# Reordering the front of a decoder layer: memory matmuls between tile 1's attention groups, queries behind them

## The chip, the cores and the metric

One Trainium2 chip, one core. The metric is the device time of one execution in microseconds (us), lower is better. TensorE (PE) works on a 128 by 128 array, with VectorE (DVE), ScalarE (ACT), GpSimd (POOL) and the DMA queue of SyncE (SP) beside it; each takes its instructions in the order in which the program issues them, and they meet at semaphores.

## The reference

A layer over 256 positions of width 1024, in two sub-layers, each closed with `LayerNorm(alpha * x + f(x))`:

```python
# mixing: one projection of x gives all heads; outputs are concatenated and projected
nsa  = g0 * attend(q, compress(k), compress(v)) + g1 * attend(q, selected blocks) + g2 * attend(q, window)
dsa  = attend(q, k, v over the 64 keys with the largest index score)
mem  = softmax(q @ mem_k.T / 8) @ mem_v          # 4 heads, 256 memory tokens
x1   = layer_norm(alpha * x + concat(nsa, dsa, mem) @ w_out)
# channel: PEER, 8 retrieval heads over 128 * 128 experts
s1, s2 = (x1 @ w_query) halves @ sub_keys ; top 16 of each, top 16 of their sums -> experts, gates
y    = sum_e gate_e * gelu(x1 @ u_e) * v_e
out  = layer_norm(alpha * x1 + y)
```

With 256 positions the selection takes all blocks and the window reaches over all keys, so both branches are plain causal attention with their own keys and values.

## The kernel before

Tokens lie in two tiles of 128 (t = 0 and 1). All matrix work of the front is float32, which the trace shows as two matrix instructions for each matmul of the program. The kernel has a **front** (projections, attention, output projection, first norm, the queries of PEER) up to about 284 us and then 128 **expert chunks** in (`expert_in`) and 128 out (`expert_out`); the change touches only the front. The order on each engine is written out by hand.

**Groups.** Attention other than the compressed branch is cut into 20 groups (`UNITS`), each at most 512 score columns wide: in tile 0 "sel" and "win" for two kv groups with four heads each, "dsa" in two halves, "mem" in two halves; in tile 1 the same with two heads a group. A group u runs through

- `scores(u)` on PE (L573 and after), which may start once `maxima(u-2)` has read the PSUM bank,
- `maxima(u)` on DVE (L1298, L1302, L1306): adds the mask and takes each row's maximum,
- `exps(u)` on ACT (L927): the exponential with its row sum,
- `normalise(u)` on DVE (L1314, L1317, L1321): multiplies by one over the sum and, for sel and win, by the gate,
- `turn(u)` on PE (L619): two or four transposes into PSUM bank 2, and `save_turn(u)` on ACT (L937) copies them out,
- `outputs(u)` on PE: probabilities times values into banks 6 and 7.

PE's loop issues `scores(u+2)`, `turn(u)`, then whatever else is laid there, then `outputs(u)`, so that the something else covers ACT's copy.

**Laid between them before.** A generator `filler` holds the last projections of tile 1 and the six memory projections `memory(0)` to `memory(5)` (queries, keys and values of the memory heads, 8 steps each); all of it is spent by the end of group 5. Then come `compress_hidden` (32 matmuls with 30 columns each, issued in one piece after `turn(6)`), `index_later` (index scores of tile 1), `compress_kv`, the compressed branch (`cmp_scores`, `cmp_turn`, `cmp_out`), the output projection of tile 0 (`mix(0)`, 16 steps of 512 columns, spread in fours over groups 9, 10, 12 and 11), the transposes of the normed tile (`turn_x1(0)`) after group 14's turn, and queries 0 to 9 beside groups 15 to 19. After group 19 follow queries 10 and 11, the output turns and `mix(1)`, queries 12 to 15, `turn_x1(1)` and queries 16 to 31. The experts start after that.

**DVE's order** follows the groups: `normalise(u)`, then `maxima(u+2)`, and between them rotary embedding of tile 1 (`rope(1)`), `compress_input`, `index_sum` (eight passes that sum the index heads, L1220), eight `index_round`s a tile that mark the top 64, the compressed softmax (`cmp_shift`, L1266 to L1272; `cmp_probs`, L1277 to L1287), the norm of tile 0, and the top 16 of sub-key scores (`subkey_tops`).

**SP** loads the query weights through a ring of 7 slots (`load_query`).

Of the kernel before, what the change touches and what calls it, by code (L numbers as in the profile page):

```python
# [19 lines left out]
KD = D // P  # L20
# [66 lines left out]
def constants():  # L87
# [8 lines left out]
    for at, half in ((0, 8), (8, 4)):  # L96
# [33 lines left out]
         + [(0, "dsa", 0, EVEN), (0, "dsa", 0, ODD), (0, "mem", 0, EVEN), (0, "mem", 0, ODD)]  # L130
         + [(1, kind, g, hs) for kind in ("sel", "win") for g in range(2) for hs in PAIRS]
# [5 lines left out]
TURNS = ([("u", u) for u in range(9)] + [("o", 0, 1), ("u", 9), ("u", 10), ("u", 11), ("o", 0, 0)]  # L137
         + [("u", u) for u in (12, 13, 14)] + [("x", 0, 0), ("x", 0, 1)] + [("u", u) for u in range(15, NU)]
         + [("o", 1, 0), ("o", 1, 1), ("x", 1, 0), ("x", 1, 1)])
QUERY_AT = 15  # L140
# [3 lines left out]
def peer_layer_kernel(nc, x, xT, memT, positions, w_tok, w_memq, w_memk, w_memv, w1k, w1v, w2k, w2v, peT,  # L144
                      w_out, ln1, wq, subk, uT, pv, ln2, consts, out):
    with ExitStack() as ctx:
# [42 lines left out]
        def small(n):  # L189
# [53 lines left out]
              rawf[:, 2048:4096].rearrange("p (i a s) -> p i a s", i=4, a=2)]  # L243
# [103 lines left out]
        def _(sp):  # L347
# [100 lines left out]
        def _(pe):  # L448
# [27 lines left out]
            def memory(m):  # L476
                a, b = m // 2, m % 2
                if m == 0:
                    pe.wait_ge(l_wmq, 16)
                    pe.wait_ge(l_mT, 16)  # L480
                    pe.wait_ge(l_wmk, 16)
                    pe.wait_ge(l_wmv, 16)
                if m < 2:
                    pe.wait_ge(h_saved, 7 + m)
                    if m == 1:
                        pe.wait_ge(gate_exp, 2)
                else:
                    pe.wait_ge(mem_saved, m - 1)
                for k in range(KD):
# [41 lines left out]
            def index_later(part):  # L531
                pe.wait_ge(tr_saved, 7)
                pe.wait_ge(mem_saved, 6)
                if part:
                    pe.wait_ge(relu_done, 6)
                for a in range(2):
                    for i in (2 * part, 2 * part + 1):
                        r = slice(32 * i, 32 * i + 32)
                        last = mm(ps[:, 4 + i % 2, a * S:(a + 1) * S], TT[r, IQ + a, P:2 * P], TT[r, IK, :],
                                  a == 0, True)  # L540
                last.then_inc(pe_idx, 1)

            def compress_hidden():
                pe.wait_ge(l_w1, 32)
                for a in range(2):
# [4 lines left out]
                    last.then_inc(pe_hid, 1)  # L550
# [71 lines left out]
            def outputs(u):  # L622
# [3 lines left out]
                if u == EARLY:  # L626
                    pe.wait_ge(mem_saved, 6)
# [87 lines left out]
            filler = chain(project(DONE[0], DONE[1]), memory(0), memory(1), memory(2), memory(3), memory(4), memory(5))  # L715
# [8 lines left out]
            for u in range(EARLY):  # L724
                if u + 2 < EARLY:
# [20 lines left out]
            for u in range(EARLY, NU):  # L746
                if u + 2 < NU:
                    scores(u + 2)
                turn(u)
                if u == 6:  # L750
                    compress_hidden()
                if u == 7:
                    index_later(0)
                if u == 8:
                    index_later(1)
                    cmp_scores(0)
                if u == 9:
                    advance(mix0, 4)
                    cmp_turn(0)
                if u == 10:  # L760
                    cmp_out(0)
                    advance(mix0, 4)
                if u == 11:
                    turn_out(0, 0)
                if u == 12:
                    advance(mix0, 4)
                if u == 14:
                    turn_x1(0)
                if u >= QUERY_AT:
                    query(2 * (u - QUERY_AT))  # L770
                    query(2 * (u - QUERY_AT) + 1)
                outputs(u)
                if u == 7:
                    compress_kv()
                if u == 8:
                    turn_out(0, 1)
                if u == 11:
                    cmp_scores(1)
                    advance(mix0, 4)
                if u == 12:  # L780
                    cmp_turn(1)
                if u == 13:
                    cmp_out(1)

            query(10)
            turn_out(1, 0)
            query(11)
# [3 lines left out]
            for j in range(12, 2 * PH):  # L791
# [73 lines left out]
        def _(act):  # L865
# [73 lines left out]
            def save_o(t, half):  # L939
                act.wait_ge(pe_pv, (4, FIRST1)[half] if t == 0 else NU)  # L940
# [44 lines left out]
            for u in range(EARLY):  # L985
# [5 lines left out]
                elif u < 4:  # L991
                    save_memory(u - 1)
                elif u == 4:
                    save_tokens(1, 0)
                    save_memory(3)
                    save_tokens(1, 1)
                    save_o(0, 0)
                else:
                    save_tokens(1, 2)
                    exps(6)  # L1000
                    save_memory(4)
                    exps(7)
                    save_memory(5)
                    save_tokens(1, 3)
            for u in range(EARLY, NU):
                save_turn(u)
                if u == 7:
                    index_relu(1, 0)
                    index_relu(1, 1)
                if u == 8:  # L1010
                    index_relu(1, 2)
                    index_relu(1, 3)
                if u == 11:
                    save_out_turn(0, 0)
                if u == 14:
                    save_x1_turn(0)
                if u + 2 < NU:
                    exps(u + 2)
                if u >= QUERY_AT:
                    save_query(2 * (u - QUERY_AT))  # L1020
                    save_query(2 * (u - QUERY_AT) + 1)
                if u == 6:
                    compress_gelu()
                if u == 7:
                    save_o(0, 1)
                if u == 8:
                    cmp_exp(0)
                    save_out_turn(0, 1)
                if u == 9:
                    save_cmp(0)  # L1030
                if u == 11:
                    cmp_exp(1)
                if u == 12:
                    save_cmp(1)
                    root(0)
            save_o(1, 0)
            save_o(1, 1)
            save_query(10)
            save_out_turn(1, 0)
            save_query(11)  # L1040
            save_out_turn(1, 1)
            for j in range(12, 4 * PH):
                if j == 14:
# [81 lines left out]
        def _(dve):  # L1125
# [271 lines left out]
            for u in range(EARLY):  # L1397
                normalise(u)
                if u + 2 < EARLY:
# [8 lines left out]
                if u == 5:  # L1408
                    maxima(6)
                    maxima(7)  # L1410
                    compress_input()
            for u in range(EARLY, NU):
                normalise(u)
                if u == 14:
                    index_bias(1)
                if u == 13:
                    norm_centre(0)
                if u + 2 < NU:
                    maxima(u + 2)
                if u == 7:  # L1420
                    compress_save()
                if u == 8:
                    cmp_shift(0)
                    index_sum(1)
                    cmp_probs(0)
                if u == 10:
# [3 lines left out]
                if 9 <= u <= 11:  # L1430
                    index_round(1)
                    index_round(1)
                if u == 11:
                    cmp_shift(1)
                if u == 12:
                    index_round(1)
# [4 lines left out]
                if u == 13:  # L1441
                    norm_scale(0)
                    index_round(1)
                if u >= QUERY_AT + 2:
                    subkey_tops(0, 2 * (u - QUERY_AT - 2), 0)

            subkey_tops(0, 6, 0)
            subkey_tops(0, 8, 0)
# [3 lines left out]
            split_x1(0)  # L1452

# [221 lines left out]
```

## Time and profile before

| | us |
|---|---|
| median of 3 runs | 1072.22 (1071.59 to 1072.44) |
| the profiled execution | 1069.4 |
| its span in the trace | 1067.6 |
| PE busy of that span | 1036.5 (97%) |
| query 16 starts | 250.87 |
| first expert chunk starts | about 284 |

The profiled execution's own time has 1.8 us beside the span, and is 2.8 us under the median. PE's clock has two levels in the trace: the granted clock 1.00 is 2.4 GHz and 0.50 is 1.2 GHz. Times below are counted from the start of the span.

### The profile page before, as it was taken

To read this page: it belongs to the slowest core of one execution; us is meant where nothing else is said; L and a number is where in the kernel's file an instruction comes from. 1 tells how busy PE (TensorE), PEld (TensorE's weight loads), DVE (VectorE), ACT (ScalarE), POOL (GpSimd) and SP (SyncE) were. 2 spreads that over 40 slices of the span, in tenths; PEclk is the share of its full clock that TensorE was granted. 3 is DMA by queue.
4 is the path that set the end of the run, shared out by engine and by line. 5 is a ranking of instruction groups with operands and counts; after the bars stand their busy time and mean duration, and the time that the engine had idled before them with its cause. 6 is when DMAs were issued, how large, how long until landed. Compare 5 with 4: busy or idle time off the path is not lost.

```text
span 1067.6 us, 17465 instructions
## 1 busy us (share of the span) xinstructions
PE 1036.5 (97%) x6508; PEld 911.3 (85%) x6508; DVE 750.8 (70%) x1818; ACT 436.8 (41%) x769; POOL 107.0 (10%) x210
## 2 busy tenths in 40 slices
PE   7998988999999999999999999999999999999996
PEld 3467855979999999999999999998888888888885
DVE  1172167438999968999999996566666666666667
ACT  1243223323344475555555554443333333333341
POOL 1000000000300023333333320000000000000000
PEclk9999569899999999999999999999999999999998
DMA  9733000338355554444444445566566555565551
GB/s 331 308 157 140 40 0 1 119 119 284 131 182 187 186 178 142 145 141 146 141 140 139 139 138 178 179 228 231 194 196 197 193 190 190 196 197 195 188 188 40
DMA packets 48611, 176.51 MB, mean 165 GB/s; under 512 B 5120, under 2 KB 6160, under 8 KB 47248
## 3 DMA queue, kind: packets, MB, share of 16 engines
q1 hardware_dynamic: 48128, 173.82, 48.3%
q0 software_dynamic: 400, 1.58, 0.5%
q8 instruction: 52, 0.85, 0.3%
q14 instruction: 31, 0.25, 0.1%
HBM read 174.33 MB, written 1.05 MB: 164 GB/s over the span
## 4 chain that ended last, share of the span: by engine, by line
PE 94%; DVE 4%; DMA 1%; issue 0%; ACT 0%; SPq 0%; DVEq 0%
PE ps L450 92%; PE ps L619 1%; DMA arena<-in_w_tok 1%; DVE slab L1220 0%; DVE arena L1321 0%; PE ps L685 0%; DVE xs L1626 0%; DVE xs L1620 0%; DVE arena L1614 0%; DVE xs L1611 0%; PE ps L520 0%; DVE arena L1247 0%; DVE arena L1302 0%; ACT arena L954 0%; DVE arena L1258 0%
## 5 line engine op out<-in xcount | busy, mean ns | idle before, releaser
L450 PE MATMUL ps<-x1hl,hi 128*128 128x256 f32 x2216 | 377.7, 285 | 0.0
L450 PEld LDWEIGHTS ps<-x1hl,hi 128*128 128x128 f32 x2216 | 327.3, 192 | 0.0
L450 PE MATMUL ps<-hi,ahl 128*128 128x512 f32 x992 | 265.3, 389 | 0.0
L450 PEld LDWEIGHTS ps<-hi,ahl 128*128 128x128 f32 x992 | 186.1, 188 | 38.6
L1095 ACT CAST hi<-slab 128x1024 fp32r<-128x1024 f32 x128 | 135.0, 1055 | 204.7 <-PE ps L450 204.6
L450 PE MATMUL ps<-x1hl,lo 128*128 128x256 f32 x688 | 194.6, 283 | 0.0
L1576 DVE TENSOR_TENSOR lo<-slab,hi 128x1024 fp32r<-128x1024 f32 x128 | 156.0, 1219 | 0.0
L450 PE MATMUL ps<-lo,ahl 128*128 128x512 f32 x496 | 152.6, 389 | 0.0
L450 PEld LDWEIGHTS ps<-x1hl,lo 128*128 128x128 f32 x688 | 131.7, 191 | 0.0
L450 PE MATMUL ps<-arena 128*128 128x128 f32 (+6 forms) x800 | 117.8, 307 | 1.4 <-ACT arena L954 0.7
L1364 DVE TENSOR_TENSOR lo<-slab,hi 128x1024 fp32r<-128x1024 f32 x86 | 106.1, 1234 | 14.1 <-ACT hi L973 14.0
L450 PEld LDWEIGHTS ps<-arena 128*128 128x128 f32 (+2 forms) x800 | 103.8, 205 | 12.0 <-issue 7.4
L973 ACT CAST hi<-slab 128x1024 fp32r<-128x1024 f32 x107 | 111.3, 1040 | 0.0
L450 PEld LDWEIGHTS ps<-lo,ahl 128*128 128x128 f32 x496 | 93.1, 188 | 19.3
L1589 DVE CAST ahl<-arena 128x256 fp32r<-128x256 f32 x124 | 36.4, 294 | 102.5 <-PE ps L450 102.5
L450 PE MATMUL ps<-arena,slab 128*128 128x512 f32 (+2 forms) x256 | 99.3, 550 | 7.4 <-DMA arena<-in_w_tok 7.4
L1060 ACT ACTIVATE gel<-ps 128x256 f32<-128x256 f32 x87 | 33.4, 384 | 147.0 <-PE ps L450 147.0
L431 POOL TENSOR_SCALAR slab<-slab,n 128x128 f32<-128x128 f32 x128 | 78.1, 622 | 151.4 <-PE ps L450 151.2
L450 PEld LDWEIGHTS ps<-arena,slab 128*128 128x128 f32 x256 | 50.6, 230 | 49.2 <-issue 39.6
L450 PE MATMUL ps<-slab 128*128 128x128 f32 (+1 forms) x576 | 82.3, 287 | 0.0
L450 PEld LDWEIGHTS ps<-slab 128*128 128x128 f32 x576 | 74.7, 192 | 2.1 <-issue 0.7
L1535 DVE TENSOR_SCALAR slab<-slab 128x128 f32<-128x128 f32 x256 | 76.0, 336 | 0.0
(199 smaller groups left out, 845.9 us busy)
## 6 DMA issues: line engine op xcount, KB each, us to landing
slab<-in_pv SPq DMA_DIRECT2D x128, 512.0 KB, 3.3
slab<-in_uT SPq DMA_DIRECT2D x107, 512.0 KB, 3.3
arena<-in_wq SPq DMA_DIRECT2D x32, 512.0 KB, 5.0
ahl_raw<-in_uT SPq DMA_DIRECT2D x21, 512.0 KB, 3.3
arena<-in_w_tok SPq DMA_DIRECT2D x2, 2048.0 KB, 16.4
arena<-in_w_out SPq DMA_DIRECT2D x1, 4096.0 KB, 13.5
arena<-in_w_tok SPq DMA_DIRECT2D x4, 512.0 KB, 8.3
arena<-in_w_tok SPq DMA_DIRECT2D x1, 1792.0 KB, 19.0
```

What stands on the lines that cost most here:

```text
L431: ins = nc.gpsimd.tensor_scalar(hot(g)[:, 0, q, :], iota, n2[:, g % 2, q:q + 1], None, ALU.is_equal)
L450: return nc.tensor.matmul(o, lhsT, rhs, start=start, stop=stop, skip_group_check=True)
L619: last = nc.tensor.transpose(ps[:, 2, b * P:(b + 1) * P], xb[u % 3][:, b * P:(b + 1) * P], ident)
L973: nc.scalar.copy(hi[:, c % UH, :], u_raw(c)).then_inc(u_hi, 1)
L1060: nc.scalar.activation(gel[:, c % 2, :], ps[:, c % 2, 0:S], ACT.Gelu).then_inc(gelu_done, 1)
L1095: nc.scalar.copy(hi[:, v_hi_slot(c), :], raw[:, v_slot(c), :]).then_inc(v_hi, 1)
L1364: v.tensor_tensor(u_rest_of(c), u_raw(c), hi[:, c % UH, :].bitcast(F32), ALU.subtract).then_inc(u_lo, 1)
L1535: ins = v.tensor_scalar(hot(g)[:, 1, q, :], iota, slotT[:, 0, tok], slotT[:, 2, tok], ALU.is_equal, ALU.mult)
L1576: v.tensor_tensor(lo[:, v_slot(c), :], raw[:, v_slot(c), :], hi[:, v_hi_slot(c), :].bitcast(F32), ALU.subtract).then_inc(v_lo, 1)
L1589: v.tensor_copy(o[:, 0, :], a).then_inc(a_hi, 1)
```

## The change

The memory groups of tile 0 move from places 6 and 7 to places 12 and 13, between tile 1's win groups; tile 1 starts at group 6. Of the memory projections only 0 and 1 stay in the filler, now taken four steps a group instead of eight. `compress_hidden` becomes a generator and alternates with `memory(2)` and `memory(3)` in groups 8 and 9, two of its matmuls for each step; `memory(4)` and `memory(5)` go whole into groups 10 and 11. Index scores of tile 1 come first (groups 6 and 7), the compressed branch later (groups 12 to 14 and 16 to 18), `mix(0)` into groups 15, 16 and 17. All queries now come after `mix(1)` and `turn_x1(0)`. ReLU results of the index scores move to two slots of the query ring, so SP holds back ring slots 5 and 6 until `index_sum(1)` has read them. ACT and DVE follow the new order.

```diff
+         + [(0, "dsa", 0, EVEN), (0, "dsa", 0, ODD)]
+         + [(1, "sel", g, hs) for g in range(2) for hs in PAIRS] + [(1, "win", 0, hs) for hs in PAIRS]
+         + [(0, "mem", 0, EVEN), (0, "mem", 0, ODD)]
+         + [(1, "win", 1, hs) for hs in PAIRS]
          + [(1, "dsa", 0, EVEN), (1, "dsa", 0, ODD), (1, "mem", 0, EVEN), (1, "mem", 0, ODD)])
-EARLY = 6
-FIRST1 = 8
+FIRST1 = 6
+MEM0 = 12
...
@@ SP
-            for j in range(RING):
+            for j in range(RING - 2):
                 load_query(j)
             sp.wait_ge(pe_hid, 2)
             sp.dma_start(ln_sb, ln1.partition_broadcast(P)).then_inc(l_ln1, 16)
-            for j in range(RING, 22):
+            sp.wait_ge(idx_read, 16)
+            for j in range(RING - 2, 22):
                 load_query(j)
...
@@ PE, groups 0 to 5
-            filler = chain(project(DONE[0], DONE[1]), memory(0), memory(1), memory(2), memory(3), memory(4), memory(5))
+            filler = chain(project(DONE[0], DONE[1]), memory(0), memory(1))
-                if u == 0:
+                if u < 4:
                     advance(filler, 4)
-                elif u < 4:
-                    advance(filler, KD)
                 elif u == 4:
                     turn_later(0)
-                    advance(filler, KD)
+                    advance(filler, 2)
                     turn_later(1)
+                    advance(filler, 2)
                 else:
                     turn_later(2)
                     scores(6)
                     advance(filler, KD)
+                    turn_later(3)
                     scores(7)
-                    advance(filler, KD)
-                    turn_later(3)
...
@@ PE, groups 6 to 19, the new order whole
+            hidden = compress_hidden()
+            keys = chain(memory(2), memory(3))
+            values = chain(memory(4), memory(5))
+            for u in range(FIRST1, NU):
                 if u + 2 < NU:
                     scores(u + 2)
                 turn(u)
                 if u == 6:
+                    index_later(0)
                 if u == 7:
                     index_later(1)
+                if u in (8, 9):
+                    for _ in range(KD):
+                        advance(hidden, 2)
+                        advance(keys, 1)
+                if u in (10, 11):
+                    advance(values, KD)
+                if u == 13:
+                    cmp_turn(0)
+                if u == 14:
+                    cmp_out(0)
+                    turn_out(0, 1)
+                if u == 15:
+                    advance(mix0, 4)
+                if u == 16:
+                    advance(mix0, 4)
+                    turn_out(0, 0)
+                if u == 17:
+                    advance(mix0, 4)
+                    cmp_turn(1)
+                if u == 18:
+                    cmp_out(1)
+                outputs(u)
+                if u == 10:
+                    compress_kv()
+                if u == 12:
                     cmp_scores(0)
+                if u == 16:
+                    cmp_scores(1)
+                if u == 17:
                     advance(mix0, 4)
...
-            query(10)
             turn_out(1, 0)
-            query(11)
             turn_out(1, 1)
             for _ in mix(1):
                 pass
-            for j in range(12, 2 * PH):
+            turn_x1(0)
+            for j in range(2 * PH):
                 query(j)
             turn_x1(1)
...
@@ DVE, groups 6 to 19
+                if u == 6:
+                    compress_input()
                 if u == 7:
+                    index_sum(1)
+                if 8 <= u <= 11:
+                    index_round(1)
+                    index_round(1)
+                if u == 11:
                     compress_save()
-                if u == 8:
+                if u == 12:
                     cmp_shift(0)
-                    index_sum(1)
                     cmp_probs(0)
...
+                if u == 16:
                     cmp_shift(1)
                     cmp_probs(1)
+                if u == 18:
                     dve.wait_ge(l_x, 16)
                     dve.wait_ge(l_ln1, 16)
                     norm_sum(0)
+                    norm_centre(0)
+                if u == 19:
                     norm_scale(0)
...
+            for b in range(0, 10, 2):
+                subkey_tops(0, b, 0)
```

## Rows read from the trace of the kernel before

**Rows 1.** The page: engines' busy time, and the granted clock in 40 slices.
```profile
PE 1036.5 (97%) x6508; PEld 911.3 (85%) x6508; DVE 750.8 (70%) x1818; ACT 436.8 (41%) x769; POOL 107.0 (10%) x210
...
PEclk9999569899999999999999999999999999999998
```

**Rows 2.** Stretches: length; busy PE, PEld, DVE, ACT, POOL; granted clock; DMA share, GB/s.
```profile
65.15:250.87 185.72, 171.62 (x917) 136.91 (x917) 89.28 (x353) 60.95 (x174) 0.00 (x0) 0.85 0.26 93
106.30:150.68 44.38, 39.15 (x153) 32.57 (x154) 16.63 (x65) 12.90 (x32) 0.00 (x0) 0.50 0.06 24
184.81:195.03 10.22, 9.54 (x40) 8.19 (x39) 2.59 (x10) 3.73 (x11) 0.00 (x0) 0.50 0.01 2
...
283.74:1067.60 783.86, 774.72 (x5128) 714.35 (x5128) 614.97 (x1246) 351.16 (x523) 103.05 (x199) 1.00 0.52 171
```

**Rows 3.** PE in order of time at the low clock: start, us, [idle before].
```profile
106.64 1.12 PE L619 MATMUL ps<-slab,arena 128*128 128x128 f32 x4 [2.66 <-DVE arena L1321]
107.54 13.70 PE L450 MATMUL ps<-arena,slab 128*128 128x30 f32 x64
121.06 3.95 PE L450 MATMUL ps<-arena 128*128 128x64 f32 x12
...
147.71 1.11 PE L619 MATMUL ps<-slab,arena 128*128 128x128 f32 x4 [3.46 <-DVE arena L1321]
148.62 4.62 PE L450 MATMUL ps<-arena,slab 128*128 128x512 f32 x8
...
191.68 5.35 PE L450 MATMUL ps<-arena 128*128 128x128 f32 x32
```

**Rows 4.** PE in order of time at the full clock.
```profile
76.68 3.62 PE L450 MATMUL ps<-slab,arena 128*128 128x256 f32 x16
80.13 1.64 PE L450 MATMUL ps<-arena 128*128 128x64 f32 x12
81.84 0.66 PE L619 MATMUL ps<-slab,arena 128*128 128x128 f32 x4
...
162.07 0.66 PE L619 MATMUL ps<-slab,arena 128*128 128x128 f32 x4
163.49 0.63 PE L658 MATMUL ps<-slab 128*128 128x128 f32 x4 [0.77 <-ACT arena L937]
163.95 1.00 PE L450 MATMUL ps<-arena 128*128 128x64 f32 x8
164.79 1.03 PE L450 MATMUL ps<-slab,arena 128*128 128x32 f32 x8
165.66 3.68 PE L450 MATMUL ps<-arena,slab 128*128 128x512 f32 x8
169.27 1.13 PE L450 MATMUL ps<-arena 64*128 64x256 f32 x4
170.33 0.66 PE L619 MATMUL ps<-slab,arena 128*128 128x128 f32 x4
...
248.26 0.60 PE L685 MATMUL ps<-slab,xs 128*128 128x128 f32 x4
...
250.87 2.05 PE L450 MATMUL ps<-arena 128*128 128x128 f32 x16 [0.68 <-ACT arena L954]
```

**Rows 5.** DVE in order of time: group 2, `compress_input`, index sum, compressed softmax.
```profile
74.97 0.69 DVE L1321 TENSOR_TENSOR arena<-arena,slab 128x512 f32<-128x512 f32 x1
...
103.84 1.95 DVE L1247 TENSOR_TENSOR arena<-arena,slab 128x240 f32<-128x240 f32 x4 [4.47 <-ACT arena L893]
...
139.68 0.35 DVE L1266 TENSOR_TENSOR arena<-ps,slab 128x60 f32<-128x60 f32 x2 [4.04 <-PE ps L450]
...
140.78 4.61 DVE L1220 SCALAR_TENSOR_TENSOR slab<-slab 128x256 f32<-128x256 f32 x8
145.41 0.28 DVE L1277 TENSOR_REDUCE slab<-arena 128x8 f32<-128x120 f32 x1
...
146.97 0.69 DVE L1321 TENSOR_TENSOR arena<-arena,slab 128x512 f32<-128x512 f32 x1
```

More of the change, by code:

```diff
@@ L129 @@
 UNITS = ([(0, kind, g, ALL4) for kind in ("sel", "win") for g in range(2)]
-         + [(0, "dsa", 0, EVEN), (0, "dsa", 0, ODD), (0, "mem", 0, EVEN), (0, "mem", 0, ODD)]
-         + [(1, kind, g, hs) for kind in ("sel", "win") for g in range(2) for hs in PAIRS]
+         + [(0, "dsa", 0, EVEN), (0, "dsa", 0, ODD)]
+         + [(1, "sel", g, hs) for g in range(2) for hs in PAIRS] + [(1, "win", 0, hs) for hs in PAIRS]
+         + [(0, "mem", 0, EVEN), (0, "mem", 0, ODD)]
+         + [(1, "win", 1, hs) for hs in PAIRS]
          + [(1, "dsa", 0, EVEN), (1, "dsa", 0, ODD), (1, "mem", 0, EVEN), (1, "mem", 0, ODD)])
 NU = len(UNITS)
-EARLY = 6
-FIRST1 = 8
+FIRST1 = 6
+MEM0 = 12
 DSA1 = 16
[L137 to L140, printed above, removed]
+TURNS = ([("u", u) for u in range(15)] + [("o", 0, 1), ("u", 15), ("u", 16), ("o", 0, 0)]
+         + [("u", u) for u in range(17, NU)] + [("o", 1, 0), ("o", 1, 1)]
+         + [("x", 0, 0), ("x", 0, 1), ("x", 1, 0), ("x", 1, 1)])
 FIRST_HI = (22, 23, 26)
@@ L532, in index_later @@
                 pe.wait_ge(tr_saved, 7)
[L533 removed]
+                pe.wait_ge(mem_saved, 2)
                 if part:
@@ L549, in compress_hidden @@
                                   flat[:, a, l, :, :].rearrange("p g b -> p (g b)"), l == 0, l == LP - 1)
-                    last.then_inc(pe_hid, 1)
+                        if l == LP - 1:
+                            last.then_inc(pe_hid, 1)
+                        yield
             def compress_kv():
@@ L723, in _ @@
             advance(filler, 6)
-            for u in range(EARLY):
-                if u + 2 < EARLY:
+            for u in range(FIRST1):
+                if u + 2 < FIRST1:
                     scores(u + 2)
                 turn(u)
-                if u == 0:
+                if u < 4:
                     advance(filler, 4)
-                elif u < 4:
-                    advance(filler, KD)
                 elif u == 4:
                     turn_later(0)
-                    advance(filler, KD)
+                    advance(filler, 2)
                     turn_later(1)
+                    advance(filler, 2)
                 else:
@@ L750, in _ @@
                 if u == 6:
-                    compress_hidden()
+                    index_later(0)
                 if u == 7:
-                    index_later(0)
-                if u == 8:
                     index_later(1)
+                if u in (8, 9):
[23 more added lines that the diff above has]
+                if u == 12:
                     cmp_scores(0)
-                if u == 9:
+                if u == 16:
+                    cmp_scores(1)
+                if u == 17:
                     advance(mix0, 4)
[L759 to L783, printed above, removed]
-            query(10)
             turn_out(1, 0)
-            query(11)
             turn_out(1, 1)
@@ L939, in save_o @@
             def save_o(t, half):
-                act.wait_ge(pe_pv, (4, FIRST1)[half] if t == 0 else NU)
+                act.wait_ge(pe_pv, (4, MEM0 + 2)[half] if t == 0 else NU)
                 nc.scalar.copy(ocs[t][:, half * 512:(half + 1) * 512], ps[:, 6 + half, :]).then_inc(o_saved, 1)
@@ L984, in _ @@
             exps(1)
-            for u in range(EARLY):
+            for u in range(FIRST1):
                 save_turn(u)
@@ L1037, in _ @@
             save_o(1, 1)
-            save_query(10)
             save_out_turn(1, 0)
-            save_query(11)
             save_out_turn(1, 1)
-            for j in range(12, 4 * PH):
-                if j == 14:
+            save_x1_turn(0)
+            for j in range(4 * PH):
+                if j == 2:
                     root(1)
@@ L1396, in _ @@
             index_round(0)
-            for u in range(EARLY):
+            for u in range(FIRST1):
                 normalise(u)
-                if u + 2 < EARLY:
+                if u + 2 < FIRST1:
                     maxima(u + 2)
@@ L1410, in _ @@
                     maxima(7)
-                    compress_input()
-            for u in range(EARLY, NU):
+            for u in range(FIRST1, NU):
                 normalise(u)
-                if u == 14:
+                if u == 13:
                     index_bias(1)
-                if u == 13:
-                    norm_centre(0)
                 if u + 2 < NU:
                     maxima(u + 2)
+                if u == 6:
+                    compress_input()
                 if u == 7:
+                    index_sum(1)
[3 more added lines that the diff above has]
+                if u == 11:
                     compress_save()
-                if u == 8:
+                if u == 12:
                     cmp_shift(0)
-                    index_sum(1)
                     cmp_probs(0)
-                if u == 10:
+                if u == 14:
                     dve.wait_ge(o_saved, 1)
@@ L1440, in _ @@
                     norm_sum(0)
-                if u == 13:
+                    norm_centre(0)
+                if u == 19:
                     norm_scale(0)
[L1443 to L1448, printed above, removed]
             norm_sum(1)
```

55 lines of the change are left out of this document (21 added, 34 removed).

## The prediction

> **What bounds the kernel now.** I read the page first: PE is busy for 97% of the span, so only what PE does, and at which clock, can move the end [rows 1]. The slices of the granted clock show the one weak place: full everywhere but in slices 5, 6 and 8, all in the front [rows 1]. The busy time by stretches says how much that is. Between turn 0 (65.15 us) and the start of query 16 (250.87 us) lie 185.72 us, of which PE is busy 171.62 and idle 14.1; two stretches of 44.38 and 10.22 us run at a granted clock of 0.50, which is 1.2 GHz, and PE is busy in them for 39.15 and 9.54 us [rows 2]. From the first expert chunk on PE is busy 774.7 of 783.9 us at full clock [rows 2]; the change leaves those instructions alone. So the question is when query 16 starts.
>
> PE in order of time says what came before each change of clock. It fell when turn 6 had waited 2.66 us for DVE, and stayed low through 64 matrix instructions with 30 columns (13.5 us, 0.211 us each) and through groups with narrow matmuls and waits; it rose inside the first dense run of 512-column steps, 2.06 us after its start at 148.62 [rows 3]. The second time it fell among waits and narrow groups and rose 3.35 us after the dense queries had begun at 191.68 [rows 2, 3]. It did not rise in the 12 instructions of 64 and 256 columns at 121.06 [rows 3]. Taken together: waits with narrow work around them lose the clock, and dense wide work brings it back after 2 to 4 us.
>
> **The work itself.** The change removes no arithmetic. At full clock the work of turn 0 to query 16 is 171.6 - (39.15 + 9.54) / 2 = 147.3 us. That halving holds for steps whose price I see at both levels: 512-column steps take 0.43 us an instruction at full clock [rows 4] and dense queries the half of what they take at low clock. For `compress_hidden` only the low level is in the trace; its nearest rows at full clock are the 32-column matmuls at 0.109 us (164.79 to 165.66) and the 64-column ones at 0.105 [rows 4], so 64 x 0.107 = 6.8 us, bounds 6.7 to 7.0. Alternating it with `memory(2)` and `memory(3)` (3.45 us each, 76.68 to 80.13 [rows 4]) I take as the plain sum, 13.7 us for both; that a wide step hides a following load could save up to 16 x 0.1 = 1.6 us, and that the switching costs as much is the other bound.
>
> **Idle places of the new order.** I laid the new order out by hand from these prices: turn 0.49 us, output of a tile 1 group 0.85, its scores 1.06, four steps of `mix(0)` 3.5, compressed scores 0.87, and 1.4 us from a turn to its output when nothing covers ACT's copy (162.07 to 163.49) [rows 4]. A place is idle where DVE or ACT is late.
> - Groups 2 and 3. PE now takes four memory steps (1.73 us) instead of eight, but DVE is the same: `normalise(2)` ends at 75.66 [rows 5] and PE is there at 74.5, idle 1.2; behind `rope(1)` turn 3 can start at 81.2, 0.6 us sooner than the 81.84 of before [rows 4], and PE is there at 79.3, idle 1.9. The first six groups end at 91.4.
> - Groups 6 and 7. ACT's last token copies and two exponentials come before `normalise(6)`, then `compress_input` (1.95 us [rows 5]) comes before `normalise(7)`: idle 1.0 and 0.5.
> - Group 8. `index_sum(1)` (4.6 us [rows 5]) stands between `maxima(9)` and `normalise(8)`; DVE ends at 104.0, PE is there at 100.9: idle 3.1. Before, the same sum stood ahead of group 9 and cost 3.46 [rows 3].
> - Groups 12 and 13. Nothing covers the copy of group 12 (0.9). `cmp_scores(0)` follows at once, and DVE does shift, probabilities and then `normalise(13)`, with ACT's exponential between: 1.2 + 0.3 + 1.3 + 0.9 = 3.7 us (139.68 to 140.86 and 145.41 to 146.66 [rows 5]), against one 1.06 us scores group on PE: idle 2.7; then 0.7 for the copy of group 13.
> - Group 17. The same chain for tile 1, again against one scores group: idle 2.75.
> - Group 19 and after. `norm_sum(0)` and `norm_centre(0)` stand ahead of `normalise(19)` (1.9), the copy is uncovered (0.9), ACT's square root and the output copies stand ahead of the two output turns (1.2 and 0.8): 4.8.
> - The two `turn_x1`, whose copies are uncovered, 1.36 each: 2.61 us from 248.26 to 250.87, as before [rows 4].
>
> Sum 22.3 us. Query 16 would start at 65.15 + 147.3 + 22.3 = 234.8 us, 16.1 us sooner, **if the clock never fell**. This is the end of the range, not the forecast.
>
> **Edits that I cost at nothing.** All queries after `mix(1)`: they are PE work either way, and counted in the 147.3; that they no longer stand beside groups 15 to 19 is paid in the idle places above. SP: ring slots 5 and 6 wait for `compress_hidden` (about 121 us) and the index sum (103), and query 5 is wanted past 205, so the wait is hidden by 80 us; if it weren't, each late weight would cost what a load takes. The u loads behind `x1_ready` and `topped` keep their distance to query 16. DVE's `subkey_tops` take 3.0 us a pair against 4.0 us of two queries, so they run along; the last pair of tile 0 ends 6 us after query 16's start (7.9 before), so the experts' first splits are not later. ACT has to wait at `save_memory(2)` and (3) for the alternation, but the exponentials that PE needs next are ahead of it.
>
> **The clock in the new order.** Four places look like those at which it fell. (A) the 3.1 us at group 8. (B) groups 12 to 14: 4.3 us idle in 9 us, with 64-column and 32-column work between, which is the picture of 177 to 187 us before. (C) the 2.75 us at group 17. (D) 4.8 us idle in 7 us at group 19. After B the dense run is `mix(0)` in group 15; the work until it is 0.5 + 0.2 + 0.85 + 1.1 + 0.5 + 0.9 + 0.45 + 0.85 + 1.1 + 0.5 = 6.95 us, which doubles, and half of the first 2.06 us of the run [rows 3] is lost too: 8.0 us. After D: 1.8 us of work doubles and 3 us of `mix(1)` run at half pace: 3.3 us. After C `mix(0)` follows at once: 0.5 + 1.2 = 1.7 us. After A follows the alternation. If that counts as dense, the clock is back in 3 to 7 us and 2.5 us are lost. I take B and D as falling, A and C as holding or cheap: 16.1 - 8.0 - 3.3 = 4.8 us gained. Profiled execution 1069.4 - 4.8 = 1064.6; the runs' median stands 2.8 us higher, so **1067.5 us**. With A and C also losing it is 1071.7, with B shorter 1062: this case's own range is 1062 to 1072.5.
>
> **Rivals.**
> 1. The clock holds at B (PE's waits fall so that they are not counted together, or `cmp_out` and the turns are dense enough). Then 16.1 less 0 to 6: 1056 to 1062, likeliest 1059. For it: from 150.68 to 184.81 the clock held over 4.4 us of scattered waits [rows 2]. Against it: there a 3.5 us dense run stood in nearly every group, and once it was missing the clock fell.
> 2. **Slower: the alternation runs at 1.2 GHz.** It falls at A and the interleaved `compress_hidden` and memory steps are not dense enough to raise it, as the 64- and 256-column groups at 121.06 were not [rows 3]; it comes back only in the pure memory steps of group 10. Then 13.7 us of alternation and 5.5 us of turns, scores and outputs double, and some 1.5 us of group 10: about 20 us. With B, D and half of C: 16.1 - 20 - 12 = -16, somewhat less since waits shrink at a slow PE: 1083 to 1090, likeliest 1086. It decides at group 8: a wait of 3.1 us is longer than the 2.66 that preceded the first fall. This is also the case in which the change doesn't do what it says, since the spreading is there to give the narrow matmuls company.
> 3. Something that I cost at nothing shows (query weights late, DVE behind at the experts, or longer waits in tile 1): 4 to 8 us more than the forecast, 1072 to 1076.
>
> A rule that speaks against the change: the Trainium skill, "TensorE: Matmul & The Clock Gate", section "A second HAM failure mode: psum-queue depth-cycling", tells of a kernel in which short idle spells between matmul groups, from cycling through PSUM banks, make the clock swing and cost throughput. The new groups 12 to 19, with one transpose bank and nothing beside it, are of that kind. This trace agrees so far: at 184.81 us the clock fell among waits of 0.7 to 1.3 us. By that rule alone rival 1 has no room; by the rows it has some.
>
> **How the numbers follow.** Forecast case 0.42, rival 1 0.22, rival 2 0.30, rival 3 0.06. A measurement of this kernel can tell about 0.2%, 2.1 us: faster is below 1070.1, slower above 1074.4. Faster: 0.22 + 0.42 x 0.7 = 0.51. Same: 0.42 x 0.3 and half of rival 3, 0.15. Slower: 0.34. For 8 in 10 the range must take in most of rival 1 and of rival 2: 1057 to 1087.
>
> **What would show it.** PE's timeline of the new kernel: idle of about 3 us ahead of turn 8, 13 and 17, each put down to DVE's `normalise`. The granted clock: full to 100 us; in the stretch of groups 8 and 9 1.00 decides against rival 2, 0.50 for it; low from about 142 to 155 and around 180. Both expert stages unchanged. Query 16 at 246 us, 235 under rival 1's best, 262 under rival 2. I am wrong if the time moves and query 16 does not, or if waits other than those named make up the idle time.

## The result and the profile after

The changed kernel takes 1085.02 us (median of 4 runs, 1084.77 to 1086.47) against 1071.91 us before; the ratio is 1.0125, with a 95% interval of 1.0107 to 1.0142. It is slower by about 13 us where 4.8 us less was forecast. The time is that of the second rival, which was worked out as 1083 to 1090, likeliest 1086; whether its sum came true as well is asked below.

The page of the changed kernel, engines' busy time and the granted clock, beside [rows 1]:

```profile
span 1083.3 us, 17464 instructions
PE 1050.3 (97%) x6508; PEld 919.2 (85%) x6508; DVE 751.0 (69%) x1818; ACT 433.3 (40%) x767; POOL 106.4 (10%) x210
...
PEclk9997577899999999999999999999999999999998
```

PE runs as many matrix instructions as before, 6508, and is busy 13.8 us longer with them. Query 16 starts at 266.58 us instead of 250.87, and from there to the end the two kernels take 816.72 and 816.73 us: the whole difference of the spans, 15.7 us, lies ahead of it. The profiled execution of the changed kernel took 1085.13 us against 1069.4. That is 15.7 us, and the medians differ by 13.1: the profiled execution before was a quick one (granted clock 0.972 over the whole span, where most executions of that kernel, at 1071 to 1072.5 us, show 0.967 to 0.969), so part of the gap between the two traces is this one execution's luck.

Stretches of the changed kernel, columns as in [rows 2]: turn 0 to query 16, then the four stretches at the low clock.

```profile
65.10:266.58 201.48, 184.90 (x917) 145.08 (x916) 94.30 (x379) 57.90 (x172) 0.00 (x0) 0.81 0.24 86
94.22:148.84 54.62, 54.42 (x187) 44.83 (x185) 19.39 (x62) 13.57 (x36) 0.00 (x0) 0.50 0.10 39
162.49:176.14 13.65, 11.24 (x40) 8.68 (x38) 7.62 (x29) 4.89 (x14) 0.00 (x0) 0.50 0.00 0
193.22:196.62 3.40, 3.29 (x7) 1.92 (x8) 1.58 (x5) 1.51 (x5) 0.00 (x0) 0.50 0.02 5
210.28:217.12 6.84, 5.37 (x12) 2.97 (x13) 1.58 (x3) 2.31 (x5) 0.00 (x0) 0.50 0.00 0
```

The account closes in three terms. PE is busy for 74.3 us at 1.2 GHz (54.42 + 11.24 + 3.29 + 5.37), against 48.7 us before [rows 2]; half of that is lost: 37.2 us against 24.3, so **12.8 us more for the clock**. Idle time is 16.6 us against 14.1, so **2.5 us more for waits**. What is left, the work at full clock, is 184.9 - 37.2 = 147.7 us against 147.3.

PE of the changed kernel in order of time, columns as in [rows 3]: where the clock fell, the first round of the alternation, and where it rose.

```profile
89.77 2.77 PE L452 MATMUL ps<-arena 64*128 64x256 f32 x12
93.34 0.66 PE L625 MATMUL ps<-slab,arena 128*128 128x128 f32 x4 [0.80 <-DVE arena L1321]
93.93 5.73 PE L452 MATMUL ps<-arena 32*128 32x256 f32 x20
...
100.63 5.98 PE L452 MATMUL ps<-arena 32*128 32x256 f32 x20
106.81 1.12 PE L625 MATMUL ps<-slab,arena 128*128 128x128 f32 x4 [0.20 <-DVE arena L1321]
107.72 0.90 PE L452 MATMUL ps<-arena,slab 128*128 128x30 f32 x4
108.43 1.20 PE L452 MATMUL ps<-slab 128*128 128x256 f32 x2
109.42 0.90 PE L452 MATMUL ps<-arena,slab 128*128 128x30 f32 x4
...
121.37 3.81 PE L452 MATMUL ps<-arena 128*128 128x64 f32 x12
...
144.32 5.86 PE L452 MATMUL ps<-slab 128*128 128x256 f32 x16
...
165.73 1.12 PE L625 MATMUL ps<-slab,arena 128*128 128x128 f32 x4 [2.16 <-DVE arena L1321]
...
193.33 1.12 PE L625 MATMUL ps<-slab,arena 128*128 128x128 f32 x4 [2.63 <-DVE arena L1321]
...
207.58 0.66 PE L625 MATMUL ps<-slab,arena 128*128 128x128 f32 x4 [1.79 <-DVE arena L1321]
```

The clock fell at 94.2 us, right behind a wait of only 0.80 us ahead of turn 6, not at group 8 where I had put place A. From there PE was never idle for more than 0.2 us, and still the clock stayed low, first through the index scores (256 columns wide, but only 32 rows of the array high) and then through the whole alternation: one half of it, from 107.72 to 121.37, took 13.65 us, 1.71 us a round of four narrow and two 256-column instructions. It rose at 148.84, 4.5 us after the pure memory steps had begun at 144.32.

### The profile page after: what moved, and what is told of

It reads as the page before. It is cut to its first block, busy times and chain, and to the rows that moved or that the text cites. A ratio compares the mean times of both kernels' runs of the same rounds, so it can differ in the third digit from the quotient of the medians.

```text
span 1083.3 us, 17464 instructions
## 1 busy us (share of the span) xinstructions
PE 1050.3 (97%) x6508; PEld 919.2 (85%) x6508; DVE 751.0 (69%) x1818; ACT 433.3 (40%) x767; POOL 106.4 (10%) x210
## 4 chain that ended last, share of the span: by engine, by line
PE 93%; DVE 4%; ACT 1%; DMA 1%; issue 0%; SPq 0%; DVEq 0%
PE ps L452 91%; PE ps L625 1%; DMA arena<-in_w_tok 1%; DVE arena L1321 0%; PE ps L664 0%; DVE xs L1623 0%; DVE xs L1617 0%; DVE arena L1611 0%; DVE xs L1608 0%; SPq L350 0%; ACT arena L960 0%; PE ps L691 0%; DVE slab L1229 0%; DVE slab L1220 0%; PE ps L524 0%
## 5 line engine op out<-in xcount | busy, mean ns | idle before, releaser
L979 ACT CAST hi<-slab 128x1024 fp32r<-128x1024 f32 x107 | 111.1, 1039 | 0.0
L452 PE MATMUL ps<-arena,slab 128*128 128x512 f32 (+2 forms) x256 | 102.2, 550 | 6.9 <-DMA arena<-in_w_tok 6.8
L452 PEld LDWEIGHTS ps<-arena,slab 128*128 128x128 f32 x256 | 54.5, 233 | 53.1 <-issue 40.6
L452 PE MATMUL ps<-slab 128*128 128x128 f32 (+1 forms) x576 | 96.3, 309 | 0.0
L1060 ACT ACTIVATE gel<-ps 128x256 f32<-128x256 f32 x87 | 33.3, 383 | 147.3 <-PE ps L452 147.3
L452 PEld LDWEIGHTS ps<-slab 128*128 128x128 f32 x576 | 79.2, 203 | 1.4
```

What stands on the lines that cost most here:

```text
L452: return nc.tensor.matmul(o, lhsT, rhs, start=start, stop=stop, skip_group_check=True)
L979: nc.scalar.copy(hi[:, c % UH, :], u_raw(c)).then_inc(u_hi, 1)
L1060: nc.scalar.activation(gel[:, c % 2, :], ps[:, c % 2, 0:S], ACT.Gelu).then_inc(gelu_done, 1)
```

## The experiments

Two questions: is the loss the clock, or the waits and the queries' new place; and what makes the clock fall and keeps it from rising. An "unused" matmul below is extra work whose result nothing reads. The baseline of each ratio is the kernel before, run beside it.

**e3: all waits ahead of turns filled.** Changed kernel, with

```diff
+            def warm(u, n):
+                pe.wait_ge(pT_saved, nth("u", u))
+                for _ in range(n):
+                    mm(ps[:, 2, :], ident, kc[:, 0:512], True, True)
...
+                if u in (2, 3):
+                    warm(u, 1)
                 turn(u)
...
+                warm(u, {6: 1, 7: 1, 8: 3, 13: 3, 17: 3, 19: 2}.get(u, 0))
                 turn(u)
```

> Changed kernel with unused 512-column matmuls in the waits ahead of turns 2, 3, 6, 7 (one each), 8, 13, 17 (three each) and 19 (two), each 0.87 us at full clock and about as long as the wait. Theory (the loss is clock, and the waits start it): the clock is held through groups 6 to 11, and mostly through 12 to 17; query 16 starts at 236 to 246 us, time 1057 to 1068. Rival (the new waits and the queries behind mix(1) cost the time themselves): little better than 1085, or worse by the added matmuls, 1083 to 1092.

1060.48 us, ratio 0.9890 (0.9867 to 0.9913). The stretch from turn 0 to the first fall of the clock:

```profile
65.10:138.30 73.20, 71.81 (x417) 57.08 (x416) 45.02 (x187) 31.75 (x95) 0.00 (x0) 1.00 0.31 123
```

The clock is full through groups 0 to 11, the alternation included; query 16 starts at 242.24 us, 24.3 us sooner than in the changed kernel, with fifteen matmuls more. So the order, the waits and the queries' place do not cost the time by themselves: the clock does.

**e2: only the wait of 0.8 us ahead of turn 6 filled** (`warm(6, 1)`, as above).

> Changed kernel with one extra 512-column matmul (0.87 us, into the transpose bank, result unused) in the wait of 0.8 us ahead of turn 6, where the clock first falls. Theory that the fall at 94 us comes from the wait with narrow work around it, and that the alternation holds a clock that is up: clock full at least to the wait at group 8 (about 104 us), then either held (about 1066) or lost there (1080 to 1083). Rival that the alternation loses the clock by itself: the fall only moves to 104 to 108 us, 1079 to 1083 too, but with no wait in front of it. If the extra matmul changes nothing the fall stays at 94 us and the time at 1085.

1085.05 us, ratio 1.0118 (1.0093 to 1.0143): as the changed kernel. But the fall has moved. PE in order of time around groups 6 to 8 of this kernel:

```profile
92.55 1.13 PE L452 MATMUL ps<-slab 128*128 128x512 f32 x2
93.51 0.60 PE L625 MATMUL ps<-slab,arena 128*128 128x128 f32 x4
...
104.01 0.63 PE L625 MATMUL ps<-slab,arena 128*128 128x128 f32 x4 [2.99 <-issue]
```

and DVE, the end of whose second row frees turn 8:

```profile
98.19 4.60 DVE L1226 SCALAR_TENSOR_TENSOR slab<-arena,slab 128x256 f32<-128x256 f32 x8
...
103.22 0.69 DVE L1327 TENSOR_TENSOR arena<-arena,slab 128x512 f32<-128x512 f32 x1
```

And the stretches on both sides of the fall:

```profile
65.10:104.60 39.50, 33.79 (x202) 26.33 (x201) 28.30 (x127) 19.87 (x62) 0.00 (x0) 1.00 0.43 174
104.64:142.18 37.54, 37.54 (x132) 32.52 (x131) 8.55 (x30) 6.58 (x18) 0.00 (x0) 0.50 0.15 56
```

With the clock full through groups 6 and 7, PE gets to turn 8 before `index_sum(1)` and `normalise(8)` are done (at 103.91, though the profile puts the wait down to "issue") and waits 2.99 us; the 3.1 us of the prediction. In the changed kernel that wait was 0.20, because PE was slow. So a second wait stood behind the first, and the clock falls there. Behind it PE is busy every one of 37.54 us at the low clock, and the alternation does not raise it. Query 16 starts at 266.55 us, as in the changed kernel (266.58): the first low stretch is 17.1 us shorter, which is worth half of that, and it is eaten by the wait of 2.99 us and by the second low stretch, which came out 10.2 us longer than in the changed kernel (155.84 to 179.72); what set its length is open.

**e5: the waits ahead of turns 6 and 8 filled** (`warm`, one and three matmuls).

> Changed kernel with unused 512-column matmuls only ahead of turns 6 (one) and 8 (three). Two theories of where the 25 us between the changed kernel and the one with all waits filled lie. Theory (the low stretch of groups 6 to 10 is nearly all of it): clock full until group 12, the alternation takes about 7.0 us a half instead of 13.65, 1063 to 1068. Rival (the later waits weigh as much): 1072 to 1078.

1064.64 us, ratio 0.9934 (0.9919 to 0.9950): 20.4 us under the changed kernel with two places mended. The clock is full from 87.0 to 141.7 us (ahead of it lies a low stretch of 3.4 us, from 83.64, which the changed kernel's trace does not have):

```profile
87.04:141.66 54.62, 53.67 (x323) 43.60 (x323) 29.72 (x105) 24.09 (x65) 0.00 (x0) 1.00 0.14 51
141.66:155.32 13.66, 11.69 (x39) 8.93 (x39) 6.38 (x27) 4.29 (x13) 0.00 (x0) 0.50 0.01 1
```

The low stretch of groups 6 to 10 makes up five sixths of the 24.5 us between the changed kernel and e3.

**e10: the same two waits filled with narrow matmuls**, four of 64 columns for each one of 512:

```diff
-                for _ in range(n):
-                    mm(ps[:, 2, :], ident, kc[:, 0:512], True, True)
+                for _ in range(4 * n):
+                    mm(ps[:, 2, 0:64], ident, kc[:, 0:64], True, True)
```

> As the run with unused matmuls ahead of turns 6 and 8, but each 512-column matmul is replaced by four of 64 columns, which keep PE busy for the same 0.85 us. Theory (what PE streams counts, not only that it isn't idle): the clock falls in groups 6 to 8 as in the changed kernel and the alternation can't raise it, 1083 to 1087. Rival (the idle time alone makes it fall): it is held as with the wide ones, 1063 to 1067.

1064.42 us, ratio 0.9917 (0.9895 to 0.9939): as e5. Here my theory fell. PE of this kernel at the two places, with the first narrow piece of the alternation behind them, which takes 0.36 us from its start to the next, against 0.71 in the changed kernel:

```profile
92.73 1.10 PE L452 MATMUL ps<-slab 128*128 128x64 f32 x8
93.68 0.61 PE L625 MATMUL ps<-slab,arena 128*128 128x128 f32 x4
...
101.15 2.89 PE L452 MATMUL ps<-slab 128*128 128x64 f32 x24
104.14 0.66 PE L625 MATMUL ps<-slab,arena 128*128 128x128 f32 x4
104.64 0.53 PE L452 MATMUL ps<-arena,slab 128*128 128x30 f32 x4
105.00 0.68 PE L452 MATMUL ps<-slab 128*128 128x256 f32 x2
```

To hold the clock over these two waits it was enough that PE wasn't idle; 64 columns did it as well as 512. To raise it, what PE runs matters, as the next two show.

**e1: memory steps ahead of `compress_hidden` instead of between.**

```diff
                 if u in (8, 9):
-                    for _ in range(KD):
-                        advance(hidden, 2)
-                        advance(keys, 1)
+                    advance(keys, KD)
+                    advance(hidden, LP)
```

> Changed kernel; in groups 8 and 9 the eight memory steps go in one piece ahead of the sixteen compress_hidden matmuls, instead of alternating. Same work. Theory (the alternation is too thin to raise the clock, dense wide steps do it in 2 to 4 us): the clock, low from about 94 us, comes back within the memory steps of group 8, around 111 us; the narrow piece behind them may lose it again. If it stays up until group 10, about 17 us less than the changed kernel, 1068; if it is lost in each narrow piece and won back in each memory piece, 5 to 10 us less, 1075 to 1080. Rival (order within the groups doesn't matter, the low stretch is set by the waits): 1085, low until about 148 us as before.

1074.49 us, ratio 1.0025 (1.0007 to 1.0043), 10.5 us under the changed kernel with the same instructions, and half a us under the 1075 to 1080 of the expectation. The stretches, cut where the clock changes:

```profile
94.58:111.64 17.06, 16.85 (x57) 12.24 (x54) 12.09 (x37) 6.66 (x19) 0.00 (x0) 0.50 0.00 1
111.64:118.48 6.84, 6.84 (x52) 6.51 (x51) 0.00 (x0) 0.37 (x1) 0.00 (x0) 1.00 0.00 0
118.48:121.88 3.40, 3.40 (x12) 2.38 (x11) 2.45 (x11) 1.55 (x5) 0.00 (x0) 0.50 0.00 0
121.88:128.72 6.84, 6.84 (x52) 6.53 (x51) 1.25 (x4) 0.95 (x3) 0.00 (x0) 1.00 0.01 2
128.72:135.54 6.82, 6.82 (x20) 5.15 (x20) 3.61 (x11) 4.04 (x10) 0.00 (x0) 0.50 0.77 308
```

The memory steps of group 8 began at 108.07 and the clock rose at 111.64; it fell again, at 118.48 and 128.72, a little behind each narrow piece of 32 instructions (113.30 to 116.8, and 124.43 to 127.9), among 64-column ones, although PE was busy without a break. Won back in each memory piece and lost in each narrow one: the second form of the expectation.

**e9: one dense piece first, then the alternation.**

```diff
+                if u == 8:
+                    advance(keys, KD)
                 if u in (8, 9):
                     for _ in range(KD):
                         advance(hidden, 2)
                         advance(keys, 1)
-                if u in (10, 11):
+                if u == 10:
                     advance(values, KD)
...
-            keys = chain(memory(2), memory(3))
-            values = chain(memory(4), memory(5))
+            keys = chain(memory(2), memory(3), memory(4))
+            values = memory(5)
```

> Changed kernel, nothing added: memory(2) goes in one piece ahead of the alternation in group 8, which then runs with memory(3) and memory(4). Theory (a dense piece raises the clock, the alternation then holds it): low from 94 us to 110 or 113 us only, then full until group 12; 17 to 20 us less than the changed kernel, 1065 to 1069. Rival (the alternation loses it again): 1074 to 1082.

1075.21 us, ratio 1.0036 (1.0023 to 1.0049). The time missed the 1065 to 1069 of the expectation and lies where the rival put it; the mechanism was that of the expectation, not of the rival:

```profile
77.42:80.84 3.42, 3.42 (x12) 2.76 (x10) 3.25 (x20) 1.25 (x5) 0.00 (x0) 0.50 1.03 443
94.48:111.56 17.08, 16.88 (x58) 12.14 (x59) 12.13 (x41) 6.86 (x19) 0.00 (x0) 0.50 0.00 1
111.56:142.28 30.72, 30.05 (x190) 26.66 (x188) 10.93 (x36) 8.84 (x24) 0.00 (x0) 1.00 0.18 69
```

The clock rose 2.2 us after `memory(2)` had begun (109.38) and stayed up through both halves of the alternation (113.92 to 130.46). What I had not counted is that group 11 had lost its memory steps: DVE's `compress_save` now stands uncovered there, PE waits 2.44 us at 145.13, and the low stretch of the later groups became 20.5 us long (142.28 to 162.76). By the lengths of the low stretches, halved, the gain of 18.8 us in the first one is followed by a loss of 6.8 in the later ones and of 1.7 at turn 2 (the first row above), so some 10 us are left; query 16 starts at 256.27, 10.3 us sooner than in the changed kernel.

**e4 and e8: the kernel before with its waits filled**, `warm` with three, one and three matmuls ahead of turns 6, 8 and 9; in e8 also a wait for bank 5 ahead of `compress_hidden`, and in it

```diff
                         last = mm(ps[:, 3, 32 * a:32 * a + 2 * NC], w1[:, a, l, :],
                                   flat[:, a, l, :, :].rearrange("p g b -> p (g b)"), l == 0, l == LP - 1)
+                        if l % 2:
+                            mm(ps[:, 5, 0:256], ident, kc[:, 0:256], True, True)
```

> Kernel before with unused 512-column matmuls in its waits ahead of turns 6 (three), 8 (one) and 9 (three). Theory: the 64 narrow matmuls of compress_hidden lose the clock by themselves, so the fall moves from 106 us to at most about 115 us and the rise stays at or before 150: 2 to 6 us less than before, 1066 to 1070. Rival (the wait alone loses it): clock full until 180 us, some 18 us less, 1054.

> Kernel before with its waits ahead of turns 6, 8 and 9 filled as in the earlier run, and an unused 256-column matmul after every second matmul of compress_hidden. Theory (company of wide matmuls holds a clock that is up): clock full from turn 0 to group 13, 22 us less for the clock and 7 us more for the added matmuls: 1056 to 1060. Rival (narrow matmuls lose it all the same): 1066 to 1072. It also prices the new order by itself: what the alternation with real work saves against this is at most the 7 us of added matmuls.

e4: 1064.26 us, ratio 0.9927 (0.9904 to 0.9949). The fall moves from 106.3 to 111.1 us, 3.5 us into the 30-column matmuls and without a wait ahead of them: the narrow piece loses the clock by itself, as expected.

```profile
107.06 0.66 PE L619 MATMUL ps<-slab,arena 128*128 128x128 f32 x4
107.56 10.47 PE L450 MATMUL ps<-arena,slab 128*128 128x30 f32 x64
```

The time came out 1.7 us under the 1066 to 1070 expected. The rows are those of an execution of 1067.64 us at a granted clock of 0.973; the three others took 1063.07 to 1064.47 us at 0.979 to 0.983, and no trace shows where they were sooner.

e8: 1065.24 us, ratio 0.9946 (0.9932 to 0.9961), against 1056 to 1060 expected. Its stretches:

```profile
65.10:133.56 68.46, 67.03 (x387) 54.93 (x387) 26.53 (x122) 25.36 (x73) 0.00 (x0) 1.00 0.33 131
133.56:143.80 10.24, 10.24 (x25) 5.87 (x25) 8.91 (x30) 2.09 (x7) 0.00 (x0) 0.50 0.01 2
174.52:188.16 13.64, 12.20 (x42) 8.89 (x41) 7.06 (x25) 4.75 (x14) 0.00 (x0) 0.50 0.00 1
```

Wide company does hold the clock through `compress_hidden`, but I had booked all 22 us of the first low stretch as won. It was (48.7 - 22.4) / 2 = 13.1 us, less 6.9 us for the sixteen added matmuls: 6.2, and 6.1 were measured (1071.34 us beside it). Here lies the one merit of the new order that the runs show: its alternation holds a clock that is up with work that has to be done anyway.

**e7: the changed kernel with the copy waits covered too.** The fills of e3 without those ahead of turns 2 and 3, and one unused 512-column matmul (`cover`, into a bank that is free) ahead of the outputs of groups 12, 13 and 19 and ahead of each output turn of tile 1.

```diff
+            def cover(bank):
+                if bank == 5:
+                    pe.wait_ge(mem_saved, 6)
+                mm(ps[:, bank, :], ident, kc[:, 0:512], True, True)
...
+                if u == 12:
+                    cover(5)
                 if u == 13:
                     cmp_turn(0)
+                    cover(5)
+                if u == 19:
+                    cover(3)
...
+            cover(3)
             turn_out(1, 0)
+            cover(3)
             turn_out(1, 1)
```

> Changed kernel with unused matmuls in the waits ahead of turns 6, 7, 8, 13, 17 and 19, and one each in the copy waits of groups 12, 13 and 19 and ahead of the two output turns. Theory: the two low stretches that were left with all waits ahead of turns filled (10.2 us at groups 12 and 13, 3.4 us at mix(1)) go too: 1060.5 less 5.1, less 1.7, less 0.7 for the matmuls taken out ahead of turns 2 and 3, that is 1053 to 1055. Rival (the added matmuls in the copy waits are themselves on the path): 1057 to 1061.

**1054.35 us**, ratio 0.9847 (0.9834 to 0.9860): 17.0 us under the kernel before (1071.34 beside it) and 31 under the changed one; the least of all. That does not show that the new order is needed for it: the kernel before was not run with all its waits filled. An estimate from e8 says that it might come as far, 1065.2 less half of the 22.4 us that PE still works at the low clock there: 1054. Turn 0 to query 16, and the one stretch at the low clock that is left:

```profile
65.10:235.95 170.85, 166.58 (x957) 126.05 (x955) 94.41 (x379) 57.85 (x172) 0.00 (x0) 0.99 0.29 102
76.68:80.10 3.42, 3.42 (x11) 2.71 (x10) 3.28 (x20) 1.36 (x5) 0.00 (x0) 0.50 1.04 450
```

Query 16 starts at 235.95 us. The prediction had 234.8 us for this order "if the clock never fell"; e7 lost 1.7 us to the clock.

## Why the prediction was wrong

**What held.** The question was when query 16 starts, and nothing behind it moved (816.7 us in both). The work at full clock was put at 147.3 us and came out at 147.7; the idle places came where they were put: 1.18 and 1.53 us ahead of turns 2 and 3 (1.2 and 1.9 worked out), 0.80 at 6 (1.0), 2.16 at 13 (2.7), 2.63 at 17 (2.75), 1.79 at 19 (1.9), and 2.99 at turn 8 as soon as the clock was kept (3.1, e2). The end of the range without clock losses, query 16 at 234.8, is e7's 235.95 less the 1.7 us of its low stretch. What I costed at nothing (ring slots, u loads, DVE's top 16, ACT's order) cost nothing.

**The step that failed** is the choice at place A, "A and C as holding or cheap", with 2.5 us as A's price if it fell and the alternation counted as dense. The clock did fall, and the alternation did not count: PE worked 54.4 us at the low clock before the pure memory steps of group 10 brought it back, a loss of 27.2 us where the forecast had none. C fell as well, for 1.6 us. That I gave rival 2 only 0.30 rests on a reading that was one-sided, and wrong in a detail: I took the 12 instructions at 121.06 for 64- and 256-column ones, but they all have 64 columns [rows 3]. The 256-column ones that didn't raise the clock came 5 us later, with 32 rows of the array at work:

```profile
125.98 3.98 PE L450 MATMUL ps<-arena 32*128 32x256 f32 x16
```

I let the fuller look of the alternation outweigh them. The runs show both halves of it: the alternation holds a clock that is up (e3, e5, e9, e10) and doesn't raise one that is down (the changed kernel, e2).

**Rival 2 had the mechanism; its number was helped by luck.** It put the loss at A at about 20 us, and it was 27.2, because the clock fell two groups sooner. Against that stand B, C and D at 9.9 us instead of 12, waits that shrank by 5.7 us, and the 2.8 us that I added for the distance of the median from the profiled execution, which the changed kernel doesn't have (1085.02 and 1085.13). Its mark for query 16, 262 us, was passed by 4.6.

**The place was wrong too.** I took only waits of the size of 2.66 us for dangerous and costed the 1.0 us at group 6 at its own length. It fell there, behind 0.80 us, in the changed kernel, in e1 and in e9. With this wait filled the clock didn't fall there (e2), not even when the filler was narrow (e10). For the time it made no difference (e2: either of the two waits is enough to lose it).

**B, C and D** lost about what was priced for a fall there, or less: 11.24 / 2 = 5.6 us against 8.0, 1.6 against 1.7 (a fall that the forecast did not count), 2.7 against 3.3. B was sized too large because I let all work until `mix(0)` run at half pace; the clock rose 1.8 us sooner, before the mix began at 177.98. The waits shrank beside a slow PE from 22.3 to 16.6 us, as rival 2 had it.

**The rule that spoke against the change** (the Trainium skill, "TensorE: Matmul & The Clock Gate", section "A second HAM failure mode: psum-queue depth-cycling": in one kernel, short idle spells between groups of matmuls made the clock swing) was read for groups 12 to 19. The trace agrees there that the clock fell among such spells (low from 162.5 to 176.1 and around 195 and 213, with idle of 0.25 to 2.63 us), though no run separates the cycling through banks from the waits. But what decided the case was the short idle spell at group 6.

## What to carry to other kernels

Where PE is busy all the time, a wait is not worth its length: ask first whether what stands behind it is dense enough to bring the clock back, since a wait of 0.80 us, with one of 3 us next in line behind it, cost some 20 us here. A short wait can be filled with an unused matmul into a free bank, even one of 64 columns; after a fall a run of wide matmuls over all 128 rows brought the clock back and the mixed stretch didn't, so such a run belongs ahead of a narrow or mixed stretch, not behind it. And when one wait is mended, the next is already there: count the waits that a PE at full pace would meet, not those that the slow trace shows.

## What the runs showed of the hardware that was not expected

- What holds the clock and what raises it differ. A mix of 30- and 256-column float32 matmuls kept 2.4 GHz for as long as it lasted (e9: 113.92 to 130.46 us, with scores and a turn between its halves), and left 1.2 GHz at 1.2 for as long as it lasted (changed kernel: 107.7 to 139.7 us, without a break in PE).
- Width alone doesn't raise it. In the changed kernel the clock stayed low through two runs of 256-column instructions that use 32 rows (5.73 us from 93.93, 5.98 from 100.63); runs of 256-column instructions with 128 rows raised it after 2.2 us (e9), 3.6 (e1) and 4.5 (changed kernel). Nor is such a run the only thing that does: in group 14 of the changed kernel it rose at 176.14, within the last of these rows. What sets them apart from the alternation is open.

```profile
172.32 1.91 PE L452 MATMUL ps<-arena 128*128 128x256 f32 x4
174.03 1.06 PE L664 MATMUL ps<-slab 128*128 128x128 f32 x4
174.88 2.67 PE L452 MATMUL ps<-arena 128*128 128x64 f32 x12
```

- Narrow matmuls lose the clock although PE is never idle: 3.5 us into the 30-column ones in e4, and in e1 among the 64-column ones that follow 3.5 us of them. Yet 2.9 us of 64-column ones held it in e10.
- A wait of 0.80 us was followed by a fall at turn 6 in all three traces that have it unfilled at full clock (changed kernel, e1, e9). The waits of 1.18 and 1.53 us ahead of turns 2 and 3 left the clock up in the changed kernel, e1 and e2, and one of them was followed by 3.4 us at 0.50 in e5, e7, e9 and e10, with the same instructions around it. So a short wait is a risk and not a certain loss, and one trace doesn't tell its price.
- The executions of one kernel can spread: e1 from 1069.6 to 1076.7 us (10 runs), e9 from 1070.0 to 1077.3 (12), against 1054.1 to 1056.2 for e7 (5) and 1084.8 to 1086.5 for the changed kernel (4), which loses the clock four times as well. Why is open.
